# State-space layer on one core: its four pairs of head groups on two PSUM banks in turn, the carried parts computed and added ahead

## The reference, cut to what matters

```python
seg = cs[..., :, None] - cs[..., None, :]
lmat = jnp.where(causal, jnp.exp(jnp.where(causal, seg, 0.0)), 0.0)
cb = jnp.einsum('bclgn,bcsgn->bcgls', cm, bm)
y_diag = jnp.einsum('bcgls,bcgels,bcsgep->bclgep', cb, lmat, xdt)
...
y_off = jnp.einsum('bclgn,bcgepn,bcgel->bclgep', cm, start_states, jnp.exp(cs))
y = y_diag + y_off + xs * d_skip.astype(f32).reshape(G, E, 1)
y = y.reshape(bsz, seq, SSD_WIDTH) * jax.nn.silu(z.astype(f32))
```

## Time and profile before

| what | us |
|---|---|
| median of 3 runs (2740.64 to 2742.75) | 2741.02 |
| the profiled execution | 2743.45 |
| its span | 2742.2 |
| PE busy in the span | 2711.7 |
| DVE busy | 1699.7 |
| ACT busy | 1307.8 |

### The profile page before, as it was taken

One profiled execution on the slowest core, in us unless ns is written; L12 is line 12 of the kernel. 1 busy time (PEld: TensorE's weight loads), 2 busy tenths in 40 slices (PEclk: granted clock), 3 DMA queues, 4 the chain that ended last, 5 costly groups with the idle time before them and its releaser, 6 DMA issues.

```text
span 2742.2 us, 39458 instructions
## 1 busy us (share of the span) xinstructions
PE 2711.7 (99%) x16390; PEld 2323.9 (85%) x16390; DVE 1699.7 (62%) x1979; ACT 1307.8 (48%) x1672; POOL 88.8 (3%) x109
## 2 busy tenths in 40 slices
PE   9999999999999999999999999999999999999998
PEld 8887778888988888888888888888888888888887
DVE  7787677645655555556555656556666656665675
ACT  6744536444454434434344546445554434443444
POOL 1034000000000000000000000000000000000001
PEclk9999999999999999999999999999999999999999
DMA  7554456555555656556565555555555555555554
GB/s 251 173 187 139 154 171 232 183 199 172 167 171 185 198 188 195 186 187 195 197 189 187 177 189 188 181 167 171 184 174 186 194 199 184 186 198 195 189 185 138
DMA packets 392128, 506.59 MB, mean 185 GB/s; under 512 B 8312, under 2 KB 284496, under 8 KB 391440
## 3 DMA queue, kind: packets, MB, share of 16 engines
q1 hardware_dynamic: 377856, 487.80, 54.7%
q10 hardware_dynamic: 14096, 16.27, 1.9%
HBM read 501.87 MB, written 2.17 MB: 184 GB/s over the span
## 4 chain that ended last, share of the span: by engine, by line
PE 93%; DVE 3%; POOL 2%; ACT 1%; issue 1%; DMA 0%; ACTq 0%; DVEq 0%; POOLq 0%
PE PS L687 40%; PE PS L718 31%; PE PS L715 16%; PE PS L956 1%; POOL slab L3125 1%; POOL slab L3122 1%; DVE wlo L2224 1%; PE PS L758 1%; PE PS L1194 0%; PE PS L1214 0%; ACT whi L1533 0%; PE PS L741 0%; PE PS L1163 0%; PE PS L894 0%; DVE slab L2356 0%
## 5 line engine op out<-in xcount | busy, mean ns | idle before, releaser
L2224 DVE TENSOR_TENSOR wlo<-raw,whi 128x1024 fp32r<-128x1024 f32 x922 | 1126.7, 1231 | 885.3 <-ACT whi L1533 882.1
L1533 ACT ACTIVATE whi<-raw 128x1024 fp32r<-128x1024 f32 x922 | 961.6, 1056 | 1115.0 <-PE PS L715 647.9
L718 PE MATMUL PS<-XX,whi 128*128 128x512 f32 (+1 forms) x3856 | 925.8, 392 | 1.3 <-ACT whi L1533 1.2
L718 PEld LDWEIGHTS PS<-XX,whi 128*128 128x128 f32 (+1 forms) x3856 | 710.6, 189 | 142.7 <-ACT whi L1533 2.3
L687 PE MATMUL PS<-whi,act 128*128 128x512 f32 x2208 | 593.2, 390 | 0.0
L715 PEld LDWEIGHTS PS<-XX,wlo 128*128 128x128 f32 (+1 forms) x3856 | 492.9, 191 | 25.5 <-DVE wlo L2224 7.0
L715 PE MATMUL PS<-XX,wlo 128*128 128x256 f32 (+1 forms) x3856 | 503.0, 283 | 5.6 <-DVE wlo L2224 5.6
L687 PEld LDWEIGHTS PS<-whi,act 128*128 128x128 f32 x2208 | 411.9, 188 | 83.8
L687 PE MATMUL PS<-wlo,act 128*128 128x512 f32 x1104 | 340.1, 389 | 0.0
L687 PE MATMUL PS<-whi,XX 128*128 128x512 f32 x1024 | 279.1, 394 | 0.2 <-issue 0.2
L687 PEld LDWEIGHTS PS<-wlo,act 128*128 128x128 f32 x1104 | 207.2, 188 | 43.6
(11 more groups left out here) (407 smaller groups left out, 1300.2 us busy)
## 6 DMA issues: line engine op xcount, KB each, us to landing
raw<-in_ffn_w SPq DMA_DIRECT2D x128, 1024.0 KB, 5.2
raw<-in_w_in SPq DMA_DIRECT2D x101, 1024.0 KB, 5.1
raw<-in_w_ffn_gate SPq DMA_DIRECT2D x44, 1024.0 KB, 4.9
raw<-in_w_ffn_up SPq DMA_DIRECT2D x44, 1024.0 KB, 4.9
raw<-in_w_ffn_down SPq DMA_DIRECT2D x44, 1024.0 KB, 5.0
raw<-in_w_out SPq DMA_DIRECT2D x32, 1024.0 KB, 5.1
raw<-in_xattn_wk SPq DMA_DIRECT2D x16, 1024.0 KB, 5.2
raw<-in_xattn_wv SPq DMA_DIRECT2D x16, 1024.0 KB, 4.9
```

Of the source, the lines that this page charges most:

```text
L718: mm = T.matmul(ps[0:wd, f, :], k.whi[:, h % 4, o:o + wd], b.x[:, kk, :], start=kk == 0, stop=stop, skip_group_check=True)
L1533: S.activation(k.whi[:, h % 4, 0:b.size], k.raw[:, t % 4, u * b.size:(u + 1) * b.size], ACT.Copy).then_inc(k.w_hi, 1)
L2224: V.tensor_tensor(k.wlo[:, h % 4, 0:b.size], k.raw[:, h // 2 % 4, u * b.size:(u + 1) * b.size], k.whi[:, h % 4, 0:b.size].bitcast(F32), AL ...
```

## The change

It puts pairs 0 and 2 on bank 6, pairs 1 and 3 on bank 7. The two carried parts are computed at once, that of group 0 behind y1 into bank 7, that of group 1 behind y2 into bank 6 once yg0 is there, and DVE adds each to `y` in a step of its own (`carried`, signals j0 and j1) ahead of the pair's own sum. PE waits for j0 ahead of y2, for j1 ahead of y4, and for yg1 ahead of y6. On DVE the sum of a pair (`summed`) stands behind the next group's D and L. The tuple `SSD_DVE`, which gives a round to each DVE step, changes with it; those of PE and ACT stay.

```diff
-SSD_DVE = (8, 9, 9, 11, 12, 13, 13, 14, 16, 16, 16, 17, 19, 19, 20, 22, 22, 23, 25, 26, 26, 27, 28, 28, 29, 29)
+SSD_DVE = (8, 9, 9, 11, 12, 14, 14, 14, 15, 15, 16, 17, 17, 19, 19, 20, 22, 22, 25, 26, 26, 27, 28, 28, 29, 29)
...
     for n in range(8):
         c, g, q = ssd_group(n)
-        if q == 0:
-            if n:
-                T.wait_ge(*sd.DVE(f"yg{n // 2 - 1}"))
-            if c > 0:
-                T.matmul(PS[:, 7, :], cT(c, g), k.ssd_st[:, g, :], start=True, stop=True)
+        bank = 6 + n // 2 % 2
+        if n in (2, 4):
+            T.wait_ge(*sd.DVE(f"j{n // 2 - 1}"))
+        if n == 6:
+            T.wait_ge(*sd.DVE("yg1"))
         T.wait_ge(*sd.DVE(f"L{n}"))
...
         mm.then_inc(sd.pe, 1)
+        if n == 2:
+            T.wait_ge(*sd.DVE("yg0"))
+        if n in (1, 2):
+            T.matmul(PS[:, 8 - n, :], cT(1, n - 1), k.ssd_st[:, n - 1, :], start=True, stop=True).then_inc(sd.pe, 1)
         yield
...
+    def carried(g):
+
+        yg = k.y[:, 1, g * 512:g * 512 + 512]
+        V.wait_ge(*sd.PE(f"ca{g}"))
+        V.wait_ge(*sd.POOL("y1"))
+        k.dve(V.tensor_tensor(hv(k.ssd_junk), hv(PS[:, 7 - g, :]), k.bc(ecs[:, 1, 8 * g:8 * g + 8], 64), ALU.mult))
+        V.tensor_tensor(yg, yg, k.ssd_junk, ALU.add).then_inc(sd.dve, 1)
+        V.wait_ge(*sd.DVE(f"j{g}"))
+
+    def summed(pair):
+
+        c, g, _ = ssd_group(2 * pair)
+        yg = k.y[:, c, g * 512:g * 512 + 512]
+        V.wait_ge(*sd.PE(f"y{2 * pair + 1}"))
+        V.wait_ge(*sd.POOL(f"y{c}"))
+        ins = V.tensor_tensor(yg, yg, PS[:, 6 + pair % 2, :], ALU.add)
+        if g == 0:
+            k.dve(ins)
+            V.wait_ge(*k.out_of_psum(k.blocks_of("tok")[0]))
+            ins = V.tensor_tensor(yg, yg, k.Z[:, c, 0:512], ALU.mult)
+        ins.then_inc(sd.dve, 1)
+        V.wait_ge(*sd.DVE(f"yg{pair}"))
```

More of the change, by code:

```diff
@@ L388, in signals @@
             sem, "ssd",
-            pe="dt cum " + names("tr", 5) + " cb st " + names("y", 8) + " " + names("tp", 8),
-            dve="sp_e sp_u da ncs xdt xdte cb D0" + "".join(
-                (f" D{n + 1}" if n < 7 else "") + f" L{n}" + (f" yg{n // 2}" if n % 2 else "") for n in range(8))
+            pe="dt cum " + names("tr", 5) + " cb st y0 y1 ca0 y2 ca1 y3 y4 y5 y6 y7 " + names("tp", 8),
+            dve="sp_e sp_u da ncs xdt xdte cb D0 D1 L0 D2 L1 j0 D3 L2 yg0 D4 L3 j1 D5 L4 yg1 D6 L5 D7 L6 yg2 L7 yg3"
             + " zg rs yn " + names("xl", 8),
@@ L855, in ssd_pe @@
             for half in (slice(0, 64), slice(64, P)):
-                mm = T.matmul(PS[half, 6, (4 * q + e) * 64:(4 * q + e) * 64 + 64], k.Ldec[n % 3][:, e, half],
+                mm = T.matmul(PS[half, bank, (4 * q + e) * 64:(4 * q + e) * 64 + 64], k.Ldec[n % 3][:, e, half],
                               k.xdt[:, c, h * 64:h * 64 + 64], start=(q == 0 and e == 0), stop=True,
@@ L2526, in decays, with masked @@
         ins.then_inc(sd.dve, 1)
[L2527 to L2530, removed]
+    def masked(n):
+        c, g, _ = ssd_group(n)
         if n < 7:
@@ L2534, in ssd_dve @@
         V.tensor_tensor(k.Ldec[n % 3], k.Ldec[n % 3], k.rep(k.cbT[:, 2 * c + g, :], 4), ALU.mult).then_inc(sd.dve, 1)
[L2535 to L2553, removed]
+    def carried(g):
[17 more added lines that the diff above has]
+        V.wait_ge(*sd.DVE(f"yg{pair}"))
+    decays(0)
+    yield
+    masked(0)
+    yield
+    masked(1)
+    yield
+    carried(0)
+    yield
+    masked(2)
+    yield
+    summed(0)
+    yield
+    masked(3)
+    yield
+    carried(1)
+    yield
+    masked(4)
+    yield
+    summed(1)
+    yield
+    masked(5)
+    yield
+    masked(6)
+    yield
+    summed(2)
+    yield
+    masked(7)
+    yield
+    summed(3)
+    yield
     V.wait_ge(*k.out_of_psum(k.blocks_of("tok")[1]))
```

## The result

The changed kernel takes 2751.35 us (median of 6 runs, 2748.82 to 2753.95), the kernel before 2741.22 us (6 runs, 2739.61 to 2742.75). The ratio is 1.0035, 95% interval 1.0025 to 1.0045: slower by 9.6 us (6.9 to 12.3); the two medians themselves lie 10.1 us apart. The forecast was slower, by 6.9 us.

What follows compares the result with a forecast made beforehand. PE was taken as the bound without slack behind 375 us. Late starts of 6.1 us plus 0.8 for the clock made 6.9 us, 2750.35 against the profiled execution, so a median of 2747.9 us; 8-in-10 range 2742.5 to 2751.0.

Steps and rivals of the forecast that it cites:

- What bounds the kernel: Behind 375 us PE is the bound without slack, so losses in rounds 13 to 22 reach the end undiminished.
- Round 14 on DVE, the wait of 2.9 us for L2; yg0: PE waits 2.9 us ahead of y2, then 0.75 us for yg0; with a 0.86 us carried part, y3 4.5 us late.
- y4 bound by the transfer: D5, ahead of y4, waits for the n = 5 DMA, 3.45 us from issue; y4 4.4 us late.
- The estimate of 2.6 us: DMA of 256 KB for n = 5 by the skill page; y4 and whole sum would be 0.85 us less.
- y5, y6: y5 waits for DVE's masks, pair 1's sum, D6 and L5; both y5 and y6 5.4 us late.
- y6 to y7, 0.7 us for the sum behind L6: Sum of pair 2 now stands in DVE work that PE waits for: 0.7 us more, 6.1 us late.
- The clock: 0.8 us: Clock falls behind the new wait at y2, slowing group 1's carried part: 0.8 us, bounds 0 and 1.7.
- The sum: Whole kernel: 6.1 us of late starts and 0.8 us of clock, 6.9 us slower.
- Rival A: At y2 PE finds L2 ready and the two banks free it: not slower, about 2737.5 us; chance 10%.
- Rival C: Clock stays low longer, or round 15's 12 matmuls fall into the low stretch: 2749.5 to 2752 us; chance 13%.
- The last gating: Moved into round 22 in place of carried operations as long: taken at nothing, bounds -1.2 to +0.5 us.

Runs made afterwards that it cites:

- e2: Changed kernel with the rounds of its first DVE steps as in the kernel before; 2747.16 us, ratio 1.0019.
- e10: Kernel before with only the sum of pair 0, D3 and L2 moved from round 13 to 14, as in the change; 2743.35 us, ratio 1.0005.
- the pair of early transfers: Transfer for n = 5 issued a round earlier, in e2 (2743.97 us) and in the kernel before (2740.85 us).
- the filled one: Changed kernel with three thrown-away 128x512 matmuls ahead of y2 and three ahead of y4; 2749.51 us, ratio 1.0025.
- e6: Kernel before with the transfer for n = 5 issued a round earlier; 2740.85 us, ratio 0.9999.
- the second set: Changed kernel run once more, unchanged, 6 runs; 2750.59 us, ratio 1.0029.
- e9: e2 with transfers for n = 5 and 7 issued earlier and sums of pairs 1 and 2 reordered; 2741.26 us, ratio 1.0002.
- e5: e2 with the transfer for n = 5 issued a round earlier; 2743.97 us, ratio 1.0006.
- e11: e9 with its four x fetches issued behind the 1st to 4th split of the SSD's output; 2739.80 us, ratio 0.9990.
- e4: Changed kernel with its four x fetches issued late, behind the 5th to 8th split of the SSD's output; 2756.71 us, ratio 1.0051.

## Why the prediction was right, and where it was short

The direction, the new wait ahead of y2 and the bound of y4 were forecast by their mechanism, and the runs bear them out. How near the total came is in part luck, by the terms below.

*What bounds the kernel.* Right. The rest behind the SSD is 2370.3 to 2370.6 us in every version that left the x fetches alone: what rounds 13 to 22 lost came out undiminished.

*Round 14 on DVE, the wait of 2.9 us for L2; yg0.* Right. y2 was forecast at 8.5 us behind y1 and came at 8.69, behind a wait of 2.90 us. With the old rounds and two banks the wait is gone (e2), with the new rounds and the old banks there is one (e10), if a smaller one: the carried part's new place adds to it.

*y4 bound by the transfer.* Right, and shown by the pair of early transfers. In the changed kernel DVE waited 5.21 us for it; it took 3.48 us from issue (3.45 used). The estimate of 2.6 us, worked out from the Trainium skill, page "DMA: Bandwidth & Descriptors", section "Anatomy of one DMA — SWDGE (gpsimd) path", does not fit these transfers: they took 3.10 to 3.55 us in all chains that show one. The page's figure is for DMAs that GpSimd issues, and these are issued by ACT, so no run here tests the figure itself.

*y5, y6.* Right to 0.1 us once the clock is filled up (23.43 against 23.5, 30.67 against 30.7).

*y6 to y7, 0.7 us for the sum behind L6.* Open. The way is 3.19 us before. In the changed order it is 5.27 us where the clock was low in it (the first profile and the filled one), and 3.11, 3.81 and 3.56 us in the other three: -0.1 to 0.6 above the kernel before, where the term has 0.7.

*The clock: 0.8 us.* The right mechanism, too small. The forecast slowed only the carried part; the low stretch reached into the 12 matmuls behind it as well (3.68 instead of 2.97 us), and in one profile (the last gating in round 23) lasted for 6.8 us. At y3 it was 1.0 to 2.4 us, so the stated bound of 1.7 was too low as well. How many low stretches there are varies: between 312 and 385 us five in the changed kernel's first profile and two in each of the three others, one in the kernel before, and two each in e6 and e10.

*The sum.* 6.9 us, where the runs say 9.6 (6.9 to 12.3) and, in the second set, 7.9 (1.0029, 1.0018 to 1.0041: 4.9 to 11.2). The profile of the second set is 7.9 us late at the dense stream. The mis-sized terms are the clock, 0.2 to 1.6 us too small, and the stretch from y7 to the dense stream, taken at nothing, which cost 3.3 us in one profile, 0.5 in the other and -0.4 in the kernel with the gating moved; what sets that stretch in one execution stays open. The range's upper end held the second median and missed the first by 0.35 us. It came that near by luck: the bounds named beside the range, 3.3 us (4.5 less 1.2) and 8.3 us (6.1 + 1.7 + 0.5) above 2741.0, give 2744.3 to 2749.3, and the stated 2742.5 to 2751.0 is 1.7 to 1.8 us wider on each side with no term for it. Both medians lie above 2749.3.

*Rival A* (the banks free PE) fell at the point named: L2 was not there when PE came. With the rounds of before, where L2 does come in time, taking the sum off y4's way by the second bank gave 0.1 us. *Rival C*, the longer low clock, is part of what happened. *The last gating*: no effect that the runs tell (2750.61 against 2751.35 and 2750.59).

## What to carry to other kernels

Where engines run in a written order, moving a step to a later slot puts it behind whatever that slot begins with: look what its engine waits for there, since here a split that had to wait for ACT stood in front of work that PE needed 2.9 us sooner. A wait that the profile puts down to one releaser may have a second that ends within a tenth; before removing the first, add up when every other input of the waiting instruction was there. And compare profiles from an event at the end of the unchanged code, not by their spans.

## What the runs showed of the hardware that was not expected

- Where PE ran many 64x64 matmuls it stopped with no releaser, and from the stops of 0.5 us and more, all but one, it went on 1.1 to 1.6 us behind the end of a 16 KB fetch on the instruction queue. With no x fetch near the stops were of 0.3 to 1.5 us, about every 3.5 us; with 512 KB fetches beside, the longest of a profile was of 2.0 to 3.4 us. A gain of 1.2 us ahead of such a stretch was gone behind it (e9).
- The length of a wait alone did not tell whether the granted clock fell to 0.50. Around the wait of 2.90 us ahead of y2 it fell in all four profiles, for 3.4 us, in one for 6.8. Ahead of y4 it fell with 1.86 us (e5, e9, e11) and with 2.93 (the kernel before), but for 5 us behind waits of 2.80 us (e2) and 3.05 us (e4) it stayed at 1.00. In the one profile with 2.7 us of thrown-away matmuls in both waits it stayed at 1.00 from 264 us up to y6.
- The start of y1 lay anywhere from 314.7 to 320.0 us in the thirteen profiles, with no change ahead of it: 314.7 to 315.8 without a low clock near 254 us, 318.1 and 318.3 with 6.8 us of it, 319.8 and 320.0 with 10.2 us. That is as much as most differences measured here.
